# The order of VectorE's steps in a pair loop with seven products: four sums together, two low parts behind them

## What is computed

```python
def _conv_ffn(h, w_up, conv_w, conv_b, w_down):
    T = h.shape[1]
    u = h @ w_up                                  # (T, 1024) @ (1024, 5632)
    pad = CONV_W // 2                             # CONV_W = 3
    up = jnp.pad(u, ((0, 0), (pad, pad), (0, 0)))
    u = sum(up[:, i:i + T] * conv_w[i] for i in range(CONV_W)) + conv_b
    a, gate = jnp.split(u, 2, axis=-1)
    return (jax.nn.silu(gate) * a) @ w_down       # (T, 2816) @ (2816, 1024)
```

## Time and profile before

| | |
|---|---|
| median of three runs | 1617.04 us (1616.11 to 1618.12) |
| profiled execution | 1614.98 us |
| its span | 1613.2 us |
| TensorE (PE) busy | 1575.6 us, 98% |
| VectorE (DVE) busy | 1279.2 us, 79% |
| ScalarE (ACT) busy | 793.4 us, 49% |
| GpSimd (POOL) busy | 381.5 us, 24% |
| granted clock of TensorE | 1.0 of full speed |
| chain that ended last | PE 77%, DVE 12%, issue 3%, ACT 3%, DMA 2% |

### The profile page before, as it was taken

How to read it: one execution, slowest core, us unless ns; L and a number is a source line. 1 busy time by engine, 2 the same in 40 slices (tenths; PEclk the granted TensorE clock), 3 DMA queues, 4 the chain that set the end, 5 groups by cost and what they waited for, 6 DMA issues and landing times.

```text
span 1613.2 us, 28313 instructions
## 1 busy us (share of the span) xinstructions
PE 1575.6 (98%) x9688; PEld 1386.5 (86%) x9688; DVE 1279.2 (79%) x2255; ACT 793.4 (49%) x1483; POOL 381.5 (24%) x302
## 2 busy tenths in 40 slices
PE   8999999999999999999999999999999999999998
PEld 6788897788899999887878889967799999997886
DVE  7876587867999999966668556988689999998575
ACT  6432235638655565533373323274665565563333
POOL 0031043001455555200000400700035455541000
PEclk9999999999999999999999999999999999999999
DMA  9343265351222222454414414736313222235451
GB/s 369 131 131 97 87 224 174 85 165 53 66 86 83 82 87 85 149 157 157 150 40 144 137 53 137 261 100 153 72 43 100 78 91 78 91 91 171 129 183 66
DMA packets 65494, 195.04 MB, mean 121 GB/s; under 512 B 15361, under 2 KB 16769, under 8 KB 65153
## 3 DMA queue, kind: packets, MB, share of 16 engines
q1 hardware_dynamic: 50114, 175.54, 35.2%
q10 hardware_dynamic: 15296, 18.39, 3.5%
HBM read 187.05 MB, written 6.85 MB: 120 GB/s over the span
## 4 chain that ended last, share of the span: by engine, by line
PE 77%; DVE 12%; issue 3%; ACT 3%; DMA 2%; ACTq 1%; DVEq 0%; SPq 0%
PE bank L2083 13%; PE bank L2084 13%; PE bank L2085 13%; PE bank L2550 9%; PE bank L2552 9%; PE bank L2551 9%; DMA raw<-in_stream 2%; DVE w_lo L1940 1%; DVE w_lo L1353 1%; PE bank L2363 1%; PE bank L2350 1%; PE bank L2105 1%; PE bank L2423 1%; PE bank L2247 1%; DVE ada_sq L1364 1%
## 5 line engine op out<-in xcount | busy, mean ns | idle before, releaser
L777 ACT ACTIVATE w_hi<-raw 128x1024 fp32r<-128x1024 f32 (+1 forms) x120 | 123.2, 1029 | 394.0 <-PE bank L2085 329.9
L1353 DVE TENSOR_TENSOR w_lo<-raw,w_hi 128x1024 fp32r<-128x1024 f32 (+1 forms) x128 | 156.9, 1231 | 166.9 <-ACT w_hi L777 166.6
L2083 PE MATMUL bank<-w_hi,aT_lo 128*128 128x512 f32 x560 | 226.3, 404 | 2.3 <-DVE aT_lo L1786 2.0
L2084 PE MATMUL bank<-w_lo,aT_hi 128*128 128x512 f32 x560 | 221.3, 395 | 0.0
L2085 PE MATMUL bank<-w_hi,aT_hi 128*128 128x512 f32 x560 | 220.9, 394 | 0.0
L2550 PE MATMUL bank<-aT_hi,w_lo 128*128 128x322 f32 x640 | 199.3, 311 | 7.8 <-DVE u L1951 4.6
L2551 PE MATMUL bank<-aT_lo,w_hi 128*128 128x322 f32 x640 | 198.7, 311 | 0.0
L2552 PE MATMUL bank<-aT_hi,w_hi 128*128 128x322 f32 x640 | 198.1, 310 | 0.0
L1251 ACT ACTIVATE w_hi<-raw 128x512 fp32r<-128x512 f32 x200 | 117.8, 627 | 93.2 <-POOL raw L660 93.2
L2083 PE MATMUL bank<-w_hi,m_lo 128*128 128x512 f32 x400 | 158.8, 397 | 2.9 <-DVE m_lo L1985 2.6
L2084 PE MATMUL bank<-w_lo,m_hi 128*128 128x512 f32 x400 | 157.3, 393 | 0.0
(11 more groups left out here) (275 smaller groups left out, 3817.1 us busy)
## 6 DMA issues: line engine op xcount, KB each, us to landing
raw<-in_stream SPq DMA_DIRECT2D x304, 512.0 KB, 3.6
lead<-in_lead SPq DMA_DIRECT2D x16, 512.0 KB, 10.5
bias<-in_bias ACTq DMA_DIRECT2D x8, 896.0 KB, 10.8
na_v<-vn ACTq DMA_DIRECT2D x2, 1280.0 KB, 5.7
x<-in_xs SPq DMA_DIRECT2D x4, 512.0 KB, 12.4
vt<-na_v ACTq DMA_DIRECT2D x16, 128.0 KB
gb_mix<-gates ACTq DMA_DIRECT2D x2, 1024.0 KB, 5.0
gb_ffn<-gates ACTq DMA_DIRECT2D x8, 256.0 KB, 4.5
```

Source lines behind the costliest of these rows:

```text
L777: act.activation(w_hi[:, g % 4, 0:n], raw[:, s % 4, 0:n], ACT.Copy).then_inc(hi_done, 1)
L1353: dve.tensor_tensor(w_lo[:, g % 4, 0:n], raw[:, s % 4, 0:n], w_hi[:, g % 4, 0:n].bitcast(F32), ALU.subtract).then_inc(raw_free[s % 4], 1)
L2083: pe.matmul(out, ll, rh, start=start, stop=False)
L2084: pe.matmul(out, lh, rl, start=False, stop=False)
```

## The change

It moves steps in the queues of VectorE and ScalarE and adds a wait on GpSimd; no instruction of work is added or removed.
- On VectorE, in each half of the loop: `first_with_sixth` moves ahead of `block_low` 6; `block_low` 1 and 0 of the following pair move behind `gate_sum`, so that the four sums stand together but for low part 6 behind the first.
- On VectorE behind the loop: `split_lo` of the third w_down granule moves from between the last two `column_conv` to behind two `down_low`.
- On ScalarE ahead of the loop: `gate_silu(None, 1)` moves behind `block_high` 2 to 5.
- On GpSimd ahead of the loop: the sum at L683 waits as well until low parts 0 to 4 of the first pair are written.

```diff
@@ -680,6 +680,7 @@
                 fourth_sum(1, 0)
                 pool.wait_ge(s_sum_done, at(s_sum_done, layer, 3))
                 pool.wait_ge(s_lo_done, at(s_lo_done, layer, 3))
+                pool.wait_ge(blk_lo, at(blk_lo, layer, 5))
                 pool.tensor_tensor(s_sum[:, 0], h_part(0, 1), s_sum[:, 1], ALU.subtract).then_inc(s_sum_done, 1)
                 gated(0, 0)
                 third_sum(1, 1)
@@ -1284,9 +1285,9 @@
                 block_high(0, 1, 1)
                 block_high(1, 1, 1)
                 s_high(3)
-                gate_silu(None, 1)
                 for n in range(2, 6):
                     block_high(n, 1, 1)
+                gate_silu(None, 1)
                 with act.Fori(1, NSP // 2) as i:
                     for e in range(2):
                         column_mid(i, e, 0)
@@ -2018,13 +2019,13 @@
                         gate_early(i, e)
                         column_conv(i, e, 0)
                         column_conv(i, e, 1)
+                        first_with_sixth(*after(i, e))
                         block_low(6, *after(i, e))
-                        block_low(1, i + 1, e)
-                        block_low(0, i + 1, e)
-                        first_with_sixth(*after(i, e))
                         with_seventh(*after(i, e))
                         gate_late(*after(i, e))
                         gate_sum(*after(i, e))
+                        block_low(1, i + 1, e)
+                        block_low(0, i + 1, e)
                         value_early(*after(i, e))
                         for n in range(2, 5):
                             block_low(n, i + 1, e)
@@ -2047,10 +2048,10 @@
                 value_late(last, 1)
                 gate_early(last, 1)
                 column_conv(last, 1, 0)
-                split_lo(W_DOWN0 + 2, layer)
                 column_conv(last, 1, 1)
                 for kt in (2, 3):
                     down_low(0, kt, m_lo[:, kt, :], m_hi[:, kt, :])
+                split_lo(W_DOWN0 + 2, layer)
                 split_lo(W_DOWN0 + 3, layer)
                 dve.wait_ge(blk_mm, at(blk_mm, layer, PROD * NSP))
                 for gi in range(G_DOWN):
```

## The result

The changed kernel takes 1666.72 us (median of 4 runs, 1665.89 to 1668.31), the kernel before on the same chip 1617.58 us (4 runs, 1616.11 to 1619.54). The ratio is 1.0304, interval 1.0286 to 1.0322: 3% slower. The forecast was 1665.0 us, range 1645 to 1682. The profiled execution of after is the highest of its four, 1668.31 us with a span of 1666.5, and it reaches the loop of layer 0 at 409.85 us, 1.47 us later than the profile of before did; times inside the loop are compared with that taken off.

The account below looks back on a forecast made before the run. TensorE bounds the kernel, but VectorE's ring of 13.86 us would exceed its 12.50; 17 rings, a longer one and the edges sum to +24.2 us a layer, +48.4 for two: 1665 us, range 1645 to 1682.

Parts of the forecast that it names:

- low 0 to low 2: VectorE in the loop: low 2 waits through third_sum and the high part of block 2, 2.84 or 2.65 us.
- value_late to the first convolution: VectorE in the loop: 2.14 us, its end set by ScalarE's two column_mid steps.
- ring: VectorE's cycle from low 0 to the next low 0, one half of the loop body: 13.86 us against TensorE's 12.50.
- last sum of pair 1: VectorE early in the loop: the sum that product 6 needs starts at 432.2, before at 435.77.
- last sum, pair 18 to 19: VectorE at the loop's end: a longer ring of 16.6 us, as low parts meet GpSimd's gated step.
- product 6 of pair 19: TensorE at the loop's end: starts at 685.0 where it started at 660.53, +24.5 us.
- Rivals 1 and 2: 1: third_sum's delay misses VectorE, 1608 us, chance 0.07. 2: ring near 12.7 balances the gains, 1615 us, chance 0.03.
- Rival 3: TensorE idles 1.4 us in each half and its clock falls for a while: 1680 us, chance 0.05.
- The wait appears on TensorE before product 6: TensorE in each half of the loop: waits before product 6 for the last sum, about 1.4 us.
- Nothing in the ring waits for TensorE: In the loop: no step of VectorE's ring is held by TensorE; the third sum's product 3 ends early enough.
- (c): Behind the loop: split_lo of the third W_down granule behind m_lo; of a 1.0 us TensorE wait, 0.3 is gained.
- 4.4 x 2 = 8.8: Gain in us if only the edges count: TensorE's waits of 3.4 and 1.0 go, in two layers.

Follow-up runs that it names:

- loop_only: The kernel before with only the loop's new VectorE order, the edits around the loop not made: 1671.19 us, ratio 1.0328.
- the three orders between: Changed kernel with low parts 1 and 0 moved to behind low part 6 (1615.8 us), behind with_seventh (1628.34 us) or behind gate_late (1648.16 us).
- edges_no_c: The loop order of before with the edits around the loop, but split_lo of the third W_down granule back between the last convolutions: 1614.85 us, ratio 0.9983.
- edges_only: Changed kernel with the loop's order put back as before, the edits around the loop kept: 1613.16 us, ratio 0.9973.
- own_buffer_old_order: Loop order of before, edits around the loop kept, third_sum writing to a free part of m: 1624.75 us, ratio 1.0042.
- own_buffer: Changed kernel, but in the loop third_sum writes to a free part of m without waiting for low parts; fourth_sum waits for both: 1639.9 us, ratio 1.0137.
- zero_first: Changed kernel with low 0 ahead of low 1; third_sum waits for low 0 alone, fourth_sum for both: 1662.57 us, ratio 1.0274.

## Why the prediction was right

Its steps against the profile of after (the loop is entered 1.47 us late; "less 1.47" is the time with that taken off):

| step | predicted | measured |
|---|---|---|
| low 0 to low 2 | 2.84 / 2.65 | 2.82 / 2.63 |
| lows 2 to 4 | 2.2 (mean) | 2.28 / 2.08 |
| value_late to the first convolution | 2.14 | 2.15 (660.95 to 663.10) / 2.23 |
| both convolutions | 3.69 | 3.68 (663.10 to 666.78) |
| first sum to low 1 | 2.48 | 2.46 |
| ring | 13.86 | 13.85 |
| last sum of pair 1 | 432.2 | 433.43, less 1.47 is 431.96 |
| last sum, pair 18 to 19 | 16.6 | 16.25 |
| product 6 of pair 19 | 685.0 | 685.86, less 1.47 is 684.39 |

The last two rows, of VectorE and then of TensorE:

```profile
668.83 0.49 DVE L1966 TENSOR_TENSOR u<-bank,u 128x322 f32<-128x322 f32 x1
...
672.47 3.53 DVE L1941 TENSOR_TENSOR w_lo<-raw,w_hi 128x512 fp32r<-128x512 f32 x3 [1.54 <-ACT w_hi L1252]
...
685.08 0.49 DVE L1966 TENSOR_TENSOR u<-bank,u 128x322 f32<-128x322 f32 x1
```

```profile
685.86 0.39 PE L2551 MATMUL bank<-aT_hi,w_lo 128*128 128x322 f32 x1 [2.50 <-DVE u L1966]
```

The ring carried the forecast, and it was right because every term of it was an instruction of the same loop, with one delay that was hidden before and whose length the trace of before already showed. loop_only and the three orders between confirm its form: the loss follows the number of sums between low 0 and low 2, and begins where the ring passes TensorE's 12.44. The ring was not luck; that the sum lies within 2 us of the measured time owes something to small errors that cancel (below).

Rivals 1 and 2 are out, since third_sum's delay reaches VectorE in each half. Rival 3, a clock that falls, is out for the profiled execution: over the longer loop it is still 1.00 (columns as above):

```profile
409.85:687.63 277.78, 261.87 (x1682) 249.06 (x1681) 233.43 (x441) 146.29 (x265) 128.00 (x96) 1.00 0.25 77
```

The stretch is 277.78 us for the same 1682 matmuls, where it was 253.92: 23.86 more. In layer 1 the loop takes 279.90 us (1224.60 to 1504.50) where before it took 254.14: 25.76 more. Together that is 49.6, against a loss of 49.1 us in the medians. The prediction took both layers as alike, at 24.2. In layer 1 the ring is 13.96, and the 0.1 us more is all in one step, value_late to the first convolution (2.31 and 2.29); why is not shown.

What was wrong, none of it large:

"The wait appears on TensorE before product 6": it stands before three products, as shown above. Once TensorE is late, the bank that the first sum reads and the next product overwrites is also wanted at once. The sum over a half is the same.

"Nothing in the ring waits for TensorE": in every second half ScalarE's first column_mid, which sets the start of the convolutions, waits last for TensorE (8 of its 16 waits from 450 to 670 us). It costs the ring little: 2.23 us in place of 2.15.

"Of the 1.0 in (c) 0.3 is left as a gain": in the changed kernel the wait before m_lo shrank to 0.44, but the next one took 1.33:

```profile
695.25 0.48 PE L2084 MATMUL bank<-w_hi,m_lo 128*128 128x512 f32 x1 [0.44 <-DVE m_lo L1986]
...
703.80 0.47 PE L2084 MATMUL bank<-w_hi,m_lo 128*128 128x512 f32 x1 [1.33 <-DVE m_lo L1986]
```

I had called the granule wanted 30 matmuls later and looked no further; the work moved behind one m_lo stands ahead of the next one. edges_no_c leaves (c) with a value that the runs can't tell from nothing.

"4.4 x 2 = 8.8" for the edges alone was mis-sized by the same step: 4.7 us measured. TensorE's wait of 2.3 us at pair 1 stays at 2.23. TensorE can gain only what VectorE gains: in edges_only the last sum of pair 1 starts at 435.02, with the loop entered at 409.71, 1.33 later than in before; less that it is 433.69, against 435.77. That is 2.1 a layer, 4.2 for two. I had added up TensorE's waits instead of asking when VectorE would be there. The sum for the changed kernel hangs on that time and not on the waits, so this error did not enter it; the ones that did, the loop's last half (0.35 us too long), the gain of (c) and layer 1's longer ring, are under 2 us and of both signs.

## What to carry to other kernels

When two steps are reordered on an engine that is not the bound, write out the ring: find who on other engines waits for the moved step, follow it back to this engine, and see what work used to lie in that distance. Ring minus the bound's period is the cost per round as soon as it is positive, and nothing before. Read the ring in every layer: in own_buffer_old_order two starts that differed by 0.1 us made it 12.49 in one layer and 12.98 in the other. Before a wait is taken from GpSimd, look at what VectorE does where the freed step will fall: beside instructions with two inputs in SBUF it is held or holds them, and that took back part of the gain in own_buffer, most of it in zero_first, and more than all of it in own_buffer_old_order.

## What the runs showed of the hardware that was not expected

A GpSimd tensor_tensor and a VectorE tensor_tensor with both inputs in SBUF do not run side by side. The prediction had taken an overlap of the two as a price of about 1 us for 1 us, on VectorE alone, from one row. The runs show that it goes by order of arrival and on both sides: GpSimd first, and a low part of 0.68 takes 1.40 or 1.60 (own_buffer), each time what GpSimd has left and 0.54 to 0.56 us; VectorE first, and a GpSimd step of 1.29 takes 1.68 (zero_first), or 3.04 when three low parts follow each other (own_buffer_old_order), so that the one held does not get in between them. VectorE's sums and convolutions, which read a PSUM bank and one tensor in SBUF, kept their 0.48 to 0.50 and 0.54 to 0.56 us throughout (450 to 640 us, in every kernel here). The Trainium skill (SBUF — State Buffer, Who interferes with whom) says that a VectorE instruction with two SBUF inputs contends with a GpSimd instruction that reads SBUF, calls what they share an exclusive lock, and says that the order of issue decides which one is blocked; these rows agree.

Second, the clock. TensorE that stands still in three pieces a half, and once for 2.50 us, kept clock 1.00 over the 277.78 us of the loop. But a wait of that size is not always free. In eight of the eleven variants the profile has, between its first 31 and its last 6 us, one or two spells at clock 0.50 (1.2 GHz in place of 2.4), each 3.41 us long but for one of 6.83. At most 1.6 us before each of them but that one TensorE had ended a wait of 1.3 to 3.3 us; the long one began within such a wait. In edges_no_c it is a wait of 2.22 us before the matmul at 433.80: from 435.25 on the matmuls start 0.27 us apart instead of 0.148, for 3.41 us, a loss of 1.5 us (the row under edges_no_c). The same wait in edges_only (433.98, 2.23 us) and those of 2.25 and 2.35 us in before had no such spell behind them, nor had the 2.50 and 2.53 us of the changed kernel. So the same wait at the same place can cost 1.5 us more in one execution than in another, and a difference of 1 to 3 us between two single profiles of these kernels says nothing about an edit until their clocks have been compared.
